# Gathered expert rows handled singly instead of in pairs, in a one-layer streaming encoder step

## The reference

```
h = RMSNorm(x);  z = h @ w_in
x = x + concat[GLA(z_gla), FoX(z_fox)] @ w_out
q = RMSNorm(x) @ w_q                        # 8 heads, two halves of 128
s = q . subkeys                             # 2 x 128 scores per head
top 16 of each half, 256 sums, top 16 -> idx, g = softmax(top)
a = gelu(sum_d u_tab[idx] * h)              # 8 heads x 16 experts = 128 per row
x = x + sum over 128 experts of (g * a) * v_tab[idx]
```

## Time and profile before

| | |
|---|---|
| median of 3 runs | 3796.26 us (3795.05 to 3800.52) |
| the profiled execution, its own time | 3800.59 us |
| its span | 3798.8 us |
| VectorE (DVE) busy | 2758.1 us, 73% |
| TensorE (PE) busy | 2868.9 us, 76% |
| ScalarE (ACT) busy | 1134.0 us, 30% |
| gathered by the software queue | 1131.10 MB in 1056 indirect DMAs |
| mean DMA rate | 334 GB/s |

### The profile page before, as it was taken

The page is one execution under the profiler, slowest core; times in us unless marked ns, Lnnn a source line. Parts: engine busy times, 40 slices in busy tenths (PEclk is TensorE's granted clock), DMA queues, the critical chain, the costliest instruction groups (busy, mean ns, idle before and its releaser), DMA issues.

```text
span 3798.8 us, 31751 instructions
## 1 busy us (share of the span) xinstructions
PE 2868.9 (76%) x8399; PEld 1478.9 (39%) x8399; DVE 2758.1 (73%) x6418; ACT 1134.0 (30%) x2404; POOL 1304.6 (34%) x1145
## 2 busy tenths in 40 slices
PE   7998997667767776777777777767876776787677
PEld 3454544533333343333333333323333333343333
DVE  5344344277688777899787798878777997877787
ACT  2333342123323422222432222233322222232122
POOL 0000000033443444344444343334344443444333
PEclk9999998778898888898798898888798888888889
DMA  4001000789999999999999999999999999999998
GB/s 186 23 23 45 23 26 19 302 341 382 393 411 387 411 392 420 374 374 375 398 420 420 414 405 382 359 375 420 387 420 417 410 416 404 411 391 416 420 405 357
DMA packets 187368, 1268.06 MB, mean 334 GB/s; under 512 B 23380, under 2 KB 24492, under 8 KB 39860
## 3 DMA queue, kind: packets, MB, share of 16 engines
q0 software_dynamic: 159488, 1131.10, 73.6%
q1 hardware_dynamic: 25348, 122.22, 8.0%
q10 hardware_dynamic: 2352, 12.72, 0.8%
HBM read 1239.08 MB, written 26.88 MB: 333 GB/s over the span
## 4 chain that ended last, share of the span: by engine, by line
DMA 25%; PE 23%; DVE 19%; issue 8%; ACT 4%; POOL 2%; DVEq 0%; SPq 0%; ACTq 0%; POOLq 0%
DMA uv_ring<-in_peer_uv,expert_index 24%; PE ps_acc L1402 15%; DVE uv_ring L1600 8%; PE ps_scores L1377 4%; DVE v_sums L1608 3%; POOL uv_ring L1090 2%; PE ps_scores L1258 1%; ACT coef_diag L1217 1%; PE ps_scores L1345 1%; DVE key_top_index L1490 1%; DVE key_scores_rest L1491 1%; DVE key_top_index L1499 1%; DVE coefficients L1592 1%; PE ps_acc L1246 1%; DVE candidates_rest L1491 1%
## 5 line engine op out<-in xcount | busy, mean ns | idle before, releaser
L1402 PE MATMUL ps_acc<-uv_ring,coef_diag 128*128 128x512 f32 x2672 | 1549.6, 723 | 791.2 <-ACT coef_diag L1217 790.4
L1090 POOL DMA_INDIRECT uv_ring<-in_peer_uv,expert_index x1056 | 1257.2, 1190 | 1744.7 <-PE ps_acc L1402 1562.0
L1600 DVE CUSTOM_DVE_ANT_0 uv_ring<-uv_ring,h_rows 128x1024 f32<-128x1024 f32 x1056 | 1290.4, 1222 | 300.4 <-DMA uv_ring<-in_peer_uv,expert_index 290.7
L1402 PEld LDWEIGHTS ps_acc<-uv_ring,coef_diag 128*128 128x128 f32 x2672 | 562.8, 226 | 1592.3 <-ACT coef_diag L1217 1060.7
L1209 ACT ACTIVATE gelu_u_dot_h<-u_dot_h 128x2 f32<-128x2 f32 x528 | 107.2, 203 | 1467.3 <-DVE u_dot_h L1600 1465.9
L1608 DVE SCALAR_TENSOR_TENSOR v_sums<-uv_ring,coefficients,v_sums 128x1024 f32<-128x1024 f32 x388 | 497.2, 1281 | 0.0
L392 PE MATMUL ps_z<-w_in,x_T 128*128 128x512 f32 x864 | 416.3, 630 | 5.6 <-DVE w_in L677 5.6
L1217 ACT ACTIVATE coef_diag<-ident_f,coefficients 128x128 f32<-128x128 f32 x636 | 240.7, 397 | 277.8 <-DVE coefficients L1592 277.7
L1377 PE MATMUL ps_scores<-weight_chunk,rows_T 128*128 128x256 f32 x1152 | 263.3, 383 | 4.6 <-issue 4.6
L1377 PEld LDWEIGHTS ps_scores<-weight_chunk,rows_T 128*128 128x128 f32 x1152 | 221.1, 192 | 67.2 <-issue 40.5
L392 PEld LDWEIGHTS ps_z<-w_in,x_T 128*128 128x128 f32 x864 | 164.9, 200 | 193.0 <-issue 181.0
(11 more groups left out here) (203 smaller groups left out, 2494.7 us busy)
## 6 DMA issues: line engine op xcount, KB each, us to landing
weight_chunk<-scratch_keys_w SPq DMA_DIRECT2D x48, 1024.0 KB, 9.1
weight_chunk<-in_w_out_chunks SPq DMA_DIRECT2D x24, 1024.0 KB, 13.4
uv_ring<-in_peer_uv,expert_index POOLq DMA_INDIRECT x1056, 11.9
w_in<-in_w_in_chunks SPq DMA_DIRECT2D x6, 2048.0 KB, 24.6
uv_ring<-in_w_peer_q_T SPq DMA_DIRECT2D x8, 1024.0 KB, 24.4
x_T<-in_x_T POOLq DMA_DIRECT2D x9, 512.0 KB, 4.7
x_rows<-in_x_rows POOLq DMA_DIRECT2D x9, 512.0 KB, 5.7
x_mid<-in_x_rows SPq DMA_DIRECT2D x9, 512.0 KB, 19.1
```

What stands on the lines that cost most here:

```text
L1090: pool.indirect_dma_start(out=ring[:, s % RING, :], out_offset=None, in_=dram["uv"], in_offset=bass.IndirectOffsetOnAxis(ap=idx[:, t % IDX ...
L1402: mm = pe.matmul(acc[:, c, :], diag[:, r, :], ring[:, r, D + c * 512:D + (c + 1) * 512], start=first, stop=False, skip_group_check=True)
L1600: dve.tensor_tensor_reduce(out=ring[:, s % RING, 0:D], in0=ring[:, s % RING, 0:D], in1=h2[:, t % 2, :], scale=1.0, scalar=0.0, op0=ALU.mul ...
```

## The change

The group size becomes 1, and the rule for VectorE's share is rewritten so that it names the same rows: row s goes to VectorE if s is odd (beside attention and projection), or if s mod 4 is 3 (elsewhere).

```diff
-RING, GRP = 8, 2
+RING, GRP = 8, 1
...
-    return 1 if BESIDE[GRP * g + GRP] else g % 2
+    return g % 2 if BESIDE[GRP * g + GRP] else g % 4 // 3
```

## The result

The change makes the kernel slower: 3955.03 us (3950.93 to 3962.09), against 3798.39 us (four runs of each), a ratio of 1.0414 (95% interval 1.0397 to 1.043). That is 157 us, nearly four times the 42 us forecast, and beyond the range.

What follows compares the result with a forecast made beforehand. VectorE was taken to bound routing stretches, the transfer mostly attention and projection. Terms 15 + 5 + 24 - 2 = 42 us made 3842 us by the profiled execution, predicted as 3840 us, range 3780 to 3900.

Steps and rivals of the forecast that it cites:

- first term: Coefficient products on VectorE double, 528 to 1056: 15 us in VectorE-bound stretches, 5 us leaking through elsewhere.
- The 83 us by the Trainium skill's rule: Fixed latency per VectorE instruction charged whole to the added products, nothing hidden, over the program: 83 us.
- second term: Rows reach TensorE at other moments, shifting key scores in routing of tiles 2 to 5: 24 us, from -10 to 40.
- a = 1: Key scores placed behind row a, with a modulo 4 being 1: never waited before, forecast 4.5 us later.
- transfer-bound stretches: Mostly attention and projection, where DMA delivery sets the pace: small additions to VectorE absorbed, 5 us leaking through.
- The count that was made for key scores: Time from VectorE's product before dot a until TensorE finishes the rows ahead of the scores; now 3.95 us for row a-1.
- the list of what would show me wrong: Signs against it: a = 1 units still not waiting, transfer-bound stretches below 410 GB/s, or 0.27 us product waits in most routing rows.
- the ring pays: Reading given to transfer-bound stretches falling below 410 GB/s: the ring, not VectorE, would pay.
- The pairs were the burden: Rival: TensorE's bursts of pair sums delay key scores, so single rows are faster, 3768 us; chance of faster 0.18.
- Full charge: Rival: gelu round trip lengthens VectorE's row in VectorE-bound stretches, lateness at its bound: 125 us, some 3920 us; chance 0.10.

Runs made afterwards that it cites:

- the two runs with TensorE one step later: TensorE's sums one step later in its own order, once against the change with single rows (3766.59 us), once against the kernel before with pairs (3749.93 us).
- the split alone: Kernel before, pairs kept, with each pair's gelu and coefficient product issued as two one-column instructions: 3815.18 us, 1.003 of before.
- the run with TensorE one step later: The change with TensorE's sums one step later (row s-2 at step s), ScalarE's order as in the change: 3766.59 us, 0.9915 of before.
- both mendings: The change with the diagonal ahead of the gelu on ScalarE and TensorE's sums one step later: 3738.73 us, 0.9835 of before.
- pairs with TensorE's order alone mended: Kernel before, pairs and ScalarE unchanged, only TensorE's sums of a pair one step later: 3749.93 us, 0.987 of before.
- the run with the diagonal first: The change with the diagonal of row s-1 issued ahead of the gelu of row s on ScalarE: 3793.78 us, 0.9986 of before.

## Why the prediction was wrong

**Its first term was right in size.** It set down 15 + 5 us for the products; single rows cost some 17 us by the two runs with TensorE one step later, and the split alone 2 to 21 us. A product does hide at the end of the instruction ahead of it: at 2100.92 us the dot starts 0.07 us behind it. The 83 us by the Trainium skill's rule did not come: 81 us of busy time were added and no such time was lost.

**Its second term was right in kind, and in size where it was applied.** It forecast that a unit whose scores stand behind a row with a = 1 modulo 4, which never waited, would wait, and three more us for four units. First maxima of the units with a = 239, 246, 253, 260 after the change:

```profile
1542.59 0.49 DVE L1486 MAX8 key_top<-key_scores 128x8 f32<-128x128 f32 x2 [1.84 <-ACT key_scores L1186]
...
1564.78 0.49 DVE L1486 MAX8 key_top<-key_scores 128x8 f32<-128x128 f32 x2 [1.26 <-ACT key_scores L1186]
...
1589.26 0.49 DVE L1486 MAX8 key_top<-key_scores 128x8 f32<-128x128 f32 x2 [6.62 <-ACT key_scores L1186]
...
1611.47 0.49 DVE L1486 MAX8 key_top<-key_scores 128x8 f32<-128x128 f32 x2 [1.24 <-ACT key_scores L1186]
```

Over the 32 units of tiles 2 to 5 the means are now 0.7 (a = 0), 4.6 (a = 1), 3.6 (a = 2) and 2.5 us (a = 3): 11.4 for four, against 8, where 11 was forecast. That is 27 us over the 32 units, against 24. Those two stretches lost 41 us; 24 and a share of the products had been set down for them. Its count took 1.98 us for a row's four records, and so left out the lower clock level, at which they took 3.78 us.

**The step that failed is the sentence that transfer-bound stretches absorb additions to VectorE**, with the 5 us for them. It held for what was added to VectorE: in rows 344 to 473 the run with TensorE one step later waits 38.2 us before the products, where the kernel before waits 12.8, and takes 352 us against 351. The change waits alike (37.3 us) and takes 378. So it did not hold for what came late from TensorE. The count that was made for key scores, up to 4.5 us later by the remainder of a, applies to attention scores in the same way, since both stand behind some row in TensorE's order; its size there was not worked out. I made it only where VectorE was the bound, and did not look at `neg_max`, whose wait grew from 50.5 to 131 us. Slack of the transfer does not cover that: before, in that stretch, VectorE waited 62.5 us of 351 for rows, in pieces of at most 3.3 us, while holes of up to 5.8 us on VectorE now hold the diagonals back, from which TensorE, the ring and the gathers all follow. 102 us were lost in the stretches with attention, where the prediction had 5. In the list of what would show me wrong, the fall of these stretches below 410 GB/s was there, and came (383), but the explanation beside it, that the ring pays, was wrong: it was TensorE's order.

**The rivals.** "The pairs were the burden" had its deciding point, that scores with a = 1 have more than 4.5 us to spare, and they had none. With both mendings single rows do reach 3739 us, below the 3768 it named, but not by its mechanism: pairs with TensorE's order alone mended reach 3750. "Full charge" named 3920 us, for the wrong reason: the 105 us more before the products are nearly harmless, as the run with the diagonal first shows with 169 us of them at the time of before.

**What stays open.** How much of the loss is TensorE's lower clock. In rows 344 to 473 TensorE waited for diagonals as follows, in the kernel before, after the change, and with TensorE one step later:

```profile
PE ps_acc L1402 <- ACT coef_diag L1217: 91.5, 43, 5.9
PE ps_acc L1402 <- ACT coef_diag L1217: 94.5, 46, 4.7
PE ps_acc L1402 <- ACT coef_diag L1217: 77.5, 39, 5.0
```

The waits grew by only 3 us with the change, while TensorE's busy time for the same matmuls grew by 24 (258.7 to 283.2 us, granted clock 0.86 to 0.80) and the stretch by 27. With TensorE one step later the clock came back to 0.84. So moving the waits in TensorE's program brings the time back, but what stands queued behind a wait and what the slower clock adds were changed together; no run held one and changed the other.

## What to carry to other kernels

When a reordering makes an engine's operand later, ask what is queued behind the instruction that waits for it, in every stretch of the program, before asking who is the bound: here a diagonal made behind one more gelu (1.5 us late in the occurrence shown) cost some 140 us through scores that had nothing to do with it. Give the engine in the middle, which works in program order, one step more distance than its producer needs; the same shift by one step was worth 1.3% to the kernel before as well. And the largest wait in a list need not be the one that costs: take it away in a run before believing it.

## What the runs showed of the hardware

- The busy time of a small VectorE instruction is no measure of its price. 528 more products of 155 ns are 81 us of busy time; the split pairs, which add them with as many gelus, took 2 to 21 us more.
- A table load on ScalarE takes 1.28 us (`ACT_TABLE_LOAD`, 143 before the gelus, 183.5 us). The Trainium skill ("ScalarE: Activation LUTs", rules for kernel authors) budgets some 2.7 us for each switch to another set; here a switch shows as one load of 1.28 us, and the gelu at 2089.66 us starts 0.01 us behind its end.
- The four matmul records of one row take 1.98 us at the higher of TensorE's two clock levels (2.4 GHz, granted clock 1.00) and 3.78 us at the lower (1.2 GHz, granted clock 0.50). In the occurrence shown the engine was idle for 2.63 us before the records at the lower level. Over the same rows the mean granted clock was 0.86 before and 0.80 after.
- One ring slot of eight is worth 55 us, 1.4%, though the DMA engines show 9 tenths in every slice of the expert stage but the first and the last.
